# An expert-choice encoder layer on one core: the final tiles go through indirect transfers that leave out the last two experts' rows

## What is computed

```python
    gate, tok = lax.top_k(jnp.swapaxes(aff, 1, 2), cap)        # each expert: its 128 tokens
    xin = h[bidx, tok]
    y = jnp.einsum('becf,efd->becd', jax.nn.silu(a) * u, w_down)
    y = y * gate[..., None].astype(y.dtype)
    return jnp.zeros_like(h).at[bidx, tok].add(y)

        x = x + expert_choice_ffn(h, w_router[l], w_gate[l], w_up[l], w_down[l])
    return rmsnorm(x, final_norm_g)
```

## Time and profile before

| | |
|---|---|
| median of 3 runs | 2695.35 us (2693.93 to 2695.49) |
| profiled execution, span | 2695.3 us |
| PE busy | 2649.9 us, 98% of the span |
| DVE busy | 2067.9 us, 77% |
| ACT busy | 1463.6 us, 54% |
| POOL busy | 559.0 us, 21% |
| HBM read / written | 727.90 MB / 99.91 MB |

### The profile page before, as it was taken

One profiled execution on the slowest core, in us unless ns is written; L12 is line 12 of the kernel. 1 busy time (PEld: TensorE's weight loads), 2 busy tenths in 40 slices (PEclk: granted clock), 3 DMA queues, 4 the chain that ended last, 5 costly groups with the idle time before them and its releaser, 6 DMA issues.

```text
span 2695.3 us, 33672 instructions
## 1 busy us (share of the span) xinstructions
PE 2649.9 (98%) x12357; PEld 2187.6 (81%) x12357; DVE 2067.9 (77%) x2578; ACT 1463.6 (54%) x1717; POOL 559.0 (21%) x805
## 2 busy tenths in 40 slices
PE   9999999999999999999999989999999999999996
PEld 7888888888888888788888878888888888888884
DVE  7775766487777667863357499999999999999886
ACT  6433221122232267743232268888888888888776
POOL 1432111211111245810010111212111111111002
PEclk9999999999999999999999999999999999999998
DMA  9687775898888766444443499999999999999998
GB/s 363 245 288 295 274 264 212 284 340 288 281 299 287 260 223 209 152 144 152 152 168 133 164 419 395 391 407 404 406 402 406 402 406 403 406 402 406 399 401 347
DMA packets 251044, 827.49 MB, mean 307 GB/s; under 512 B 30326, under 2 KB 55429, under 8 KB 227853
## 3 DMA queue, kind: packets, MB, share of 16 engines
q1 hardware_dynamic: 210528, 685.12, 66.8%
q0 software_dynamic: 40352, 140.23, 15.0%
HBM read 727.90 MB, written 99.91 MB: 307 GB/s over the span
## 4 chain that ended last, share of the span: by engine, by line
PE 91%; DMA 3%; DVE 2%; ACT 2%; issue 1%; POOL 1%; SPq 0%; DVEq 0%; POOLq 0%; ACTq 0%
PE ps L3271 26%; PE ps L2902 6%; PE ps L2901 6%; PE ps L2900 6%; PE ps L2896 4%; PE ps L2898 4%; PE ps L3116 4%; PE ps L2897 4%; PE ps L3118 4%; PE ps L3117 4%; PE ps L3302 4%; PE ps L3301 4%; PE ps L3300 4%; PE ps L2951 1%; PE ps L2839 1%
## 5 line engine op out<-in xcount | busy, mean ns | idle before, releaser
L2729 DVE TENSOR_TENSOR elo<-eraw,ehi 128x2048 fp32r<-128x2048 f32 x384 | 876.6, 2297 | 79.5 <-ACT ehi L1814 71.2
L1814 ACT ACTIVATE ehi<-eraw 128x2048 fp32r<-128x2048 f32 x384 | 733.2, 1920 | 213.9 <-PE ps L3271 132.6
L1442 ACT ACTIVATE whi<-raw 128x1024 fp32r<-128x1024 f32 x159 | 168.6, 1060 | 583.2 <-PE ps L2902 240.2
L3271 PE MATMUL ps<-ehi,xh 128*128 128x512 f32 x960 | 375.1, 391 | 0.0
L3271 PE MATMUL ps<-elo,xh 128*128 128x512 f32 x960 | 373.7, 389 | 0.0
L1932 DVE TENSOR_TENSOR wlo<-raw,whi 128x1024 fp32r<-128x1024 f32 x159 | 194.6, 1224 | 187.4 <-ACT whi L1442 186.6
L3271 PE MATMUL ps<-ehi,xl 128*128 128x512 f32 x960 | 256.6, 389 | 0.0
L3271 PEld LDWEIGHTS ps<-ehi,xl 128*128 128x128 f32 x960 | 180.2, 188 | 37.5
L3271 PEld LDWEIGHTS ps<-ehi,xh 128*128 128x128 f32 x960 | 180.2, 188 | 37.2
L3271 PEld LDWEIGHTS ps<-elo,xh 128*128 128x128 f32 x960 | 180.2, 188 | 37.0
L1700 ACT ACTIVATE ohi<-oraw 128x512 fp32r<-128x512 f32 x128 | 80.7, 631 | 237.9 <-PE ps L3118 237.8
(11 more groups left out here) (500 smaller groups left out, 5431.4 us busy)
## 6 DMA issues: line engine op xcount, KB each, us to landing
raw<-in_w_stream SPq DMA_DIRECT2D x271, 512.0 KB, 5.0
eraw<-in_w_gate SPq DMA_DIRECT2D x256, 512.0 KB, 8.0
eraw<-in_w_up SPq DMA_DIRECT2D x256, 512.0 KB, 10.5
eraw<-in_w_down SPq DMA_DIRECT2D x128, 1024.0 KB, 11.6
oraw<-in_w_stream SPq DMA_DIRECT2D x128, 256.0 KB, 2.6
xt<-in_xT SPq DMA_DIRECT2D x48, 256.0 KB, 4.3
scr_ops<-xt POOLq DMA_DIRECT2D x48, 256.0 KB, 3.1
nav<-scr_rows SPq DMA_DIRECT2D x128, 64.0 KB
```

The costliest lines, as they stand in the source:

```text
L1442: act.activation(whi[:, c % SPL, :], raw_pair(c)[0], ACT.Copy).then_inc(S["w_hi"], 1)
L1814: act.activation(ehi[:, p % ERING, :], flat2(eraw[:, 2 * (p % EDEEP):2 * (p % EDEEP) + 2, :]), ACT.Copy)\
L2729: dve.tensor_tensor(elo[:, p % ERING, :], flat2(eraw[:, 2 * (p % EDEEP):2 * (p % EDEEP) + 2, :]), ehi[:, p % ERING, :].bitcast(F32), ALU.s ...
L3271: last = pe.matmul(gu_bank(e, c), a[:, k, :], w[:, p % ERING, c * BW:(c + 1) * BW], start=(k == 0 and a is hi and w is ehi), stop=(k == KD ...
```

## The change

- A new column table `kept_rows` holds, for each of the eight tiles, the row numbers of the tile; where a row belongs to expert 14 or 15, 1024 times the number of these experts that have it is added, which is out of bounds. Loads (`fetch_rows`) and stores (`store_normed`) of the tiles become indirect DMAs on POOL with this table and skip such rows.
- To make the table, PE turns the tokens of expert 14 too (one more transpose, now behind k 10 of gu 14), POOL makes `row_ids` once, and DVE compares 256 turned tokens with each tile's row numbers and counts (`find_rows`, eight instructions: four at step gu 14, k 13, and four at k 14). `overlap` moves to k 12. At k 15 `row_lists` makes both lists.
- PE's product d 13 now waits for `one_hot` at ten instead of one, which is `same`, `shared` and all eight of `find_rows`.
- `FINISH` puts the redo piece of expert 14 fifth, ahead of tile 4. POOL issues each piece's store behind the `row_scale` of the piece two places later. `write_again` waits for its own norm only.
- The wait for all that is written moves from POOL to SP.

```diff
-FINISH = tuple(range(TT + 2))
+FINISH = (0, 1, 2, 3, TT, 4, 5, 6, 7, TT + 1)
...
-            sp.wait_ge(S["scattered"], BEFORE["scattered"] + 16 * REDO)
             sp.wait_ge(S["gu_ready"], BEFORE["gu_ready"] + NE)
-            fetch_rows(0)
             sp.dma_start(gbc[:, :], t["g_final"].partition_broadcast(P)).then_inc(S["rc_in"], 16)
-            for T in range(1, TT):
-                fetch_rows(T)
-            for T in range(TT):
-                store_normed(T)
             sp.wait_ge(S["h_out0"], 16 * TT)
+            sp.wait_ge(S["scattered"], BEFORE["scattered"] + 16 * NE)
...
+            def fetch_rows(T):
+
+                if T == 0:
+                    pool.wait_ge(S["gu_ready"], BEFORE["gu_ready"] + NE)
+                    pool.wait_ge(S["one_hot"], BEFORE["one_hot"] + TT + 6)
+                else:
+                    pool.wait_ge(S["e_lo"], NP - EDEEP + 1 if T == 1 else NP - EDEEP + T + 1)
+                pool.indirect_dma_start(out=final_rows(T), out_offset=None, in_=t["x1"],
+                                        in_offset=bass.IndirectOffsetOnAxis(ap=kept_rows[:, T:T + 1].bitcast(U32), axis=0),
+                                        bounds_check=SEQ - 1, oob_is_err=False)\
+                    .then_inc(heldsem[T] if T < 4 else stsem[T - 4], 16)
+
+            def store_normed(T):
+
+                pool.wait_ge(S["r_norm"], BEFORE["r_norm"] + FINISH.index(T) + 1)
+                pool.indirect_dma_start(out=t["out"], out_offset=bass.IndirectOffsetOnAxis(ap=kept_rows[:, T:T + 1].bitcast(U32), axis=0),
+                                        in_=final_rows(T), in_offset=None, bounds_check=SEQ - 1, oob_is_err=False)\
+                    .then_inc(S["h_out0"], 16)
...
             gather_again(0)
+            fetch_rows(0)
+            fetch_rows(1)
             pool.wait_ge(S["e_lo"], NP - EDEEP + 2)
             gather_again(1)
-            for at in range(TT + 2):
-                row_scale(at)
-            pool.wait_ge(S["h_out0"], 16 * TT)
-            pool.wait_ge(S["one_hot"], BEFORE["one_hot"] + 4)
-            write_again(0)
-            write_again(1)
-            pool.wait_ge(S["scattered"], BEFORE["scattered"] + 16 * NE)
+            for T in range(2, TT):
+                fetch_rows(T)
+            row_scale(0)
+            row_scale(1)
+            for at, T in enumerate(FINISH):
+                if at + 2 < TT + 2:
+                    row_scale(at + 2)
+                if T < TT:
+                    store_normed(T)
+                else:
+                    write_again(T - TT)
...
+            def find_rows(T):
+
+                if T == 0:
+                    dve.wait_ge(S["place_consts"], BEFORE["place_consts"] + 7)
+                    dve.wait_ge(S["summed"], BEFORE["summed"] + 4 * (NE - 2))
+                if T >= 4:
+                    dve.wait_ge(S["one_hot"], BEFORE["one_hot"] + T - 1)
+                dve.tensor_scalar(out=marks[:, T % 2, 2 * P * (T // 2 % 2):2 * P * (T // 2 % 2 + 1)], in0=list_bank(NE - 1)[:, P:3 * P],
+                                  scalar1=row_ids[:, T:T + 1], scalar2=None, op0=ALU.is_equal, op1=ALU.add,
+                                  accum_out=in_last[:, T:T + 1]).then_inc(S["one_hot"], 1)
...
-                if kind == "gu" and e == NE - 2 and k == 13:
+                if kind == "gu" and e == NE - 2 and k == 12:
                     overlap()
+                if kind == "gu" and e == NE - 2 and 12 < k < 15:
+                    for T in range(4 * (k - 13), 4 * (k - 13) + 4):
+                        find_rows(T)
+                if kind == "gu" and e == NE - 2 and k == 15:
+                    row_lists()
...
-                    if e == NE - 2 and k == 12:
+                    if e == NE - 2 and k == 10:
                         last_tokens()
...
                 if e == NE - 3:
-                    pe.wait_ge(S["one_hot"], BEFORE["one_hot"] + 1)
+                    pe.wait_ge(S["one_hot"], BEFORE["one_hot"] + TT + 2)
```

More of the change, by code:

```diff
@@ L316, in trunk @@
         shared, first_only, first_rows = place(20576, ("shared", [P, 1]), ("first_only", [P, 1]), ("first_rows", [P, 1]))
+        row_ids, in_last, kept_f, kept_rows = place(20672, ("row_ids", [P, TT]), ("in_last", [P, TT]), ("kept_f", [P, TT]), ("kept_rows", [P, TT]))
         square, = place(111104, ("square", [P, D]))
@@ L1393, in _ @@
                     place_ranks(e + 1)
+                if e == 4:
+                    pool.iota(row_ids[:, :], [[P, TT]], base=0, channel_multiplier=1, allow_small_or_imprecise_dtypes=True)\
+                        .then_inc(S["place_consts"], 1)
             add_outputs(NE - 3)
@@ L2713, in overlap, with row_lists @@
                 dve.tensor_reduce(shared[:, :], same[:, :], axis=AX.X, op=ALU.max).then_inc(S["one_hot"], 1)
-                dve.wait_ge(S["one_hot"], BEFORE["one_hot"] + 2)
+            def find_rows(T):
[7 more added lines that the diff above has]
+                                  accum_out=in_last[:, T:T + 1]).then_inc(S["one_hot"], 1)
+            def row_lists():
+                dve.wait_ge(S["one_hot"], BEFORE["one_hot"] + TT + 2)
                 dve.scalar_tensor_tensor(out=first_only[:, :], in0=shared[:, :], scalar=float(SEQ), in1=tokf[:, REDO:REDO + 1],
                                          op0=ALU.mult, op1=ALU.add).then_inc(S["one_hot"], 1)
-                dve.wait_ge(S["one_hot"], BEFORE["one_hot"] + 3)
+                dve.scalar_tensor_tensor(out=kept_f[:, :], in0=in_last[:, :], scalar=float(SEQ), in1=row_ids[:, :],
+                                         op0=ALU.mult, op1=ALU.add).then_inc(S["one_hot"], 1)
+                dve.wait_ge(S["one_hot"], BEFORE["one_hot"] + TT + 4)
                 dve.tensor_copy(first_rows[:, :].bitcast(U32), first_only[:, :]).then_inc(S["one_hot"], 1)
+                dve.tensor_copy(kept_rows[:, :].bitcast(U32), kept_f[:, :]).then_inc(S["one_hot"], 1)
             for n in range(4):
@@ L3230, in last_tokens @@
                 pe.wait_ge(S["placed"], BEFORE["placed"] + NE)
+                pe.transpose(list_bank(NE - 1)[:, 2 * P:3 * P], tokf[:, NE - 2:NE - 1].to_broadcast([P, P]), ident[:, :])
                 pe.transpose(list_bank(NE - 1)[:, P:2 * P], tokf[:, NE - 1:NE].to_broadcast([P, P]), ident[:, :]).then_inc(S["same_row"], 1)
```

15 lines of the change are left out of this document (3 added, 12 removed).

## The result

The changed kernel takes 2709.20 us (median of 4 runs, 2708.01 to 2710.06) against 2695.42 for the kernel before in the same session: 1.0048 times as long, 95% interval 1.0036 to 1.0060. It is slower by 13.8 us where 6.2 were forecast, and lies 2.2 us above the range.

A forecast was written before the change was run, and what follows sets the result against it. The prediction took PE, busy 98% of the span, as the bound, up to a closing chain of waits on POOL. Terms +4.5 + 1.2 + 5.2 - 4.7 = +6.2 on 2695.3 gave 2701.5 us, range 2694.0 to 2707.0.

The forecast's parts named there:

- Term 1: Head of product d 13: PE stands idle waiting for DVE's eight find_rows comparisons, +4.5 us.
- Term 2: Behind PE's new idle time: TensorE's clock may fall to half, taken as +1.2 us, between nothing and 3.5.
- Terms 3 and 4: POOL at the end: loads delay the first norm 0.5 us; stores between row_scales stretch norm cycles to 3.8; net +5.2 us.
- Term 5: End of kernel: POOL's 6.53 us drain starts at the last issue without waiting for the landing, -4.7 us.
- Rival A: End of kernel: the drain waits for the landing, so the end is landing plus 7.0, 2706.2 us; chance 0.23.
- Rival B: POOL's stores in the ten norms do not wait for DVE: cycle 2.8 us, end at 2694.5; chance 0.20.
- Rival C: At d 13 PE does not wait, so terms 1 and 2 vanish: 2695.8 us; chance 0.12.
- term 4: POOL's indirect stores between the row_scales that DVE's norms wait for: 3.8 us a norm instead of 2.3, net +5.2 us.

The follow-up runs named there:

- e5_fill18: The changed kernel with 18 small products of the identity on PE ahead of its wait in front of d 13: 2706.62 us, ratio 1.0035.
- e7_last: The kernel of e3_spread with POOL issuing all ten row_scales first, then the eight stores and two late writes: 2706.30 us, ratio 1.0036.
- e1_sp_end: The kernel before with one edit, the wait for all that is written moved from POOL to SP: 2691.83 us, ratio 0.9987.
- e8_one: The kernel before with only tile 7 stored indirectly by POOL, one comparison, late writes freed of that tile, SP waiting for the end: 2691.09 us, ratio 0.9979.
- e6_direct: The kernel of e3_spread with the eight tile stores as plain DMAs from the same places on POOL, late writes behind all eight: 2696.39 us, ratio 0.9999.
- e3_spread: The changed kernel with overlap at k 10, the eight comparisons spread over k 10 to 12, row_lists behind k 2 of gu 15: 2700.98 us, ratio 1.0019.
- e9_one_pool: The kernel of e8_one with POOL instead of SP waiting at the end for the last late write: 2694.53 us, ratio 0.9994.

## Why the prediction was right or wrong

The direction was right, with the mechanisms of four of the five terms. The size was not. Against the sum of +6.2 the profiled pair shows +13.0, and the 6.8 us between split as follows.

- **Term 1, +4.5: right.** 4.62 us of idling, and 977.4 to 982.0 in the table. The comparisons' pace and the low part between the groups were as taken from the rows.
- **Term 2, +1.2: mechanism right, size off by 1.0.** The half clock cost 2.1 to 2.2 us (1091.9 against 1089.7 in e5_fill18, 2.1 of it behind the start of d 13). The choice "near the shorter stretch, because dense matmuls follow at once" failed: the clock fell during the idle time and stayed low for the first 4.4 us of work behind it (2553.65 to 2558), half of which is the 2.2. The upper bound of 3.5 held.
- **Terms 3 and 4, +5.2: mechanism right, off by 1.2.** The first norm waited 0.54 us for its `row_scale`, 0.6 with the gap before it (107.8 against 107.1 from d 13 to the first norm, in the kernels with and without loads on POOL), against the 0.5 forecast. The cycle is the norm's 2.35, 0.90 to the store's end, 0.58 for the `row_scale` and 0.06 between them: 3.89 and not 3.8, six times over (+0.5). At the end the last late write starts 0.8 us behind the last norm's end (2697.44 against 2696.64), not 0.3, and is done 4.1 us behind that norm's start, not 3.6 (+0.5).
- **Term 5, -4.7: wrong, and the largest miss, 2.9 us.** The failed step is "This takes the drain's length to be its own, for at 2688.5 nothing was left to land." That nothing was left to land showed only how long the drain takes when it begins late. With transfers under way it ends 3.2 us behind the last landing, 3.9 with 16 more DMAs from POOL, and having had 11.8 us instead of 5.8 makes no difference (e7_last). "SP's wait for the landing costs nothing on top" fell with it. Nor is the length fixed: 6.53 us became 7.84 with 16 more DMAs from POOL. And the forecast took the last write's 5.7 us from issue to landing over from the earlier trace rows, but it took 6.7 after the change. It is 5.7 again in e1_sp_end and 6.4 in e8_one, which has one store more ahead of it; no run isolates the reason.
- **The execution itself, 1.6.** The forecast stood on one execution whose experts began 1.6 us earlier than those of the execution after, and it took the span of that execution, 2695.3, for the time of a run; by the 1.7 us that lie between the two, that run's time was about 2697.0. In the changed kernel's runs the time is 1.7 us over the span, 2710.06 against 2708.3. The profiled execution is 0.9 above the median there. So of the 7.7 us between 2701.5 and the median of 2709.2, 6.8 are the items of this list, and about 0.8, to rounding, lies between a span and the median (1.7 - 0.9).

**Rival A** (the drain waits for the landing) was half right. The end is tied to the landing, but with 4.1 us behind it, 3.9 of them the drain, not 7.0. The forecast and this rival were the ends of a scale, and neither was given a middle; the true tail, 9.9, lies between the forecast's 7.0 and the rival's 11.7 (2700.5 - 2688.8, counted like the others from the last issue's end). The landing that was 1.0 later than both took it is 1.0 of that.

**Rival B** (stores don't wait for DVE) fell: 3.10 us beside a norm with both large inputs on chip, 0.96 with DVE idle (e7_last). The Trainium skill, SBUF — State Buffer, § Who interferes with whom, reports that `tensor_tensor` instructions did not stall a GpSimd-issued DMA, and infers why: they take only the read interface of the shared ports, and descriptor writing needs the write interface. By this case that holds beside the norm, which also has two inputs on chip, for a plain DMA (0.57 us beside the norm, e6_direct) and not for an indirect one. The same section says that a VectorE instruction with two such inputs contends with a GpSimd instruction that reads on-chip memory, and an indirect DMA is one, if its row numbers are read that way; the measurements fit this.

**Rival C** (PE does not wait) did not occur in the changed kernel; e3_spread builds it, by placing the comparisons earlier: 2700.98 us. Even then the change is slower than the kernel before, ratio 1.0019, because term 4 is larger than what the tail gives.

The traffic that the change saves showed nothing in the time. The page counts 823.51 MB in the packets of the changed kernel against 827.49 before, and the same 823.51 in e3_spread, which has no wait on PE and is still slower than before.

## What to carry to other kernels

Before a DMA is turned from plain to indirect, look at what DVE does at that moment and at what stands behind the DMA on POOL: here most cost 3.1 us instead of 1.0 beside a norm, and DVE's next input was queued behind it. Free only the dependence that ends last. One tile of eight, with one comparison instead of eight, brought what the whole table of rows was for: 26.1 us from the first norm to the last issue, where it was 28.4 to 29.0. Most of e8_one's ratio of 0.9979 comes from SP's wait, though, which alone gives 0.9987 (e1_sp_end); the freed tile without it gives 0.9994, which its interval does not tell from 1 (e9_one_pool). And a duration that was only ever seen with its neighbour already finished says nothing of what is left of it when the neighbour is moved: bound it from both sides, and take neither end as the forecast without a reason.

## What the runs showed of the hardware

- **POOL's drain at the end** takes 6.53 us (before) or 6.61 (e9_one_pool) if it begins at the last landing, and ends 3.2 behind the landing if it begins earlier. With 16 more DMAs from POOL the two numbers are 7.84 and 3.9. In both cases about half can lie beside transfers and the rest did not, even where there were 11.8 us for it (e7_last). The waited length grew by 1.31 us for 16 DMAs and by 0.08 for one, 0.08 each. What the drain does in either half no run shows.
- **Issuing from POOL** cost 0.53 to 0.64 us for a plain store, 0.96 to 1.05 for an indirect one with DVE idle or on an operand in PSUM, and up to 3.1 when it began beside a DVE instruction with two large on-chip inputs, ending 0.9 us behind that. A `row_scale`, 0.58 us alone, waited for such instructions too.
- **TensorE's clock** fell to 1.2 GHz in an idle time of 4.6 us, stayed there for 4.4 us of work behind it and cost 2.1 to 2.2 us; 18 small products of the identity in the same place held it at 2.4 GHz, with an idle rest of 0.43 us behind them.
- **The start of the expert stretch** differs by up to 3.4 us between executions of one kernel, while what lies between that start and the first norm repeats to 1.0 us and the tail to 0.1.
